# Weight rounding, bank numbers, negated maxima and product buffer of a hybrid trunk kernel rearranged

## What is computed

```python
def mixing_block(h, w_in, mix_out_gain, w_out, ...):
    proj = h @ w_in                                    # 1024 -> all four groups
    u_s5, p_ml, p_rw, p_mb = split_cols(proj, (GW, ML_COLS, RW_COLS, MB_COLS))
    y_s5 = s5_mixer(u_s5, ...)       # complex diagonal scan; y = Re(C x), GLU behind it
    y_ml = mlstm_mixer(p_ml, ...)    # row maxima m, exp(score - m), exp(-m) as a floor
    y_rw = rwkv7_mixer(p_rw, ...)    # token shift of r, k, v; delta rule in time
    y_mb = moba_mixer(p_mb, rel_bias)
    y = rms_norm(jnp.concatenate([y_s5, y_ml, y_rw, y_mb], axis=-1) by group)
    return y @ w_out

def cross_attention(h, mem_n, wq, wkv, wo):
    q = h @ wq
    kv = mem_n @ wkv                                   # mem_n = rms_norm(mem)
    return softmax(q k^T) v @ wo

x = x + rms_norm(mixing_block(rms_norm(x), ...))
x = x + rms_norm(cross_attention(rms_norm(x), rms_norm(mem), ...))
x = x + rms_norm(swiglu(rms_norm(x), ...))
```

## Time and profile before

| | |
|---|---|
| median of 3 runs | 480.02 us |
| lowest, highest | 479.83, 480.71 us |
| the profiled execution | 479.55 us |
| its span in the profile | 477.7 us |
| TensorE busy | 467.7 us (98%) |
| VectorE, ScalarE, GpSimd busy | 345.0, 272.5, 108.4 us |
| mean granted clock of TensorE | 0.997 |

### The profile page before, as it was taken

The page is one execution under the profiler, slowest core; times in us unless marked ns, Lnnn a source line. Parts: engine busy times, 40 slices in busy tenths (PEclk is TensorE's granted clock), DMA queues, the critical chain, the costliest instruction groups (busy, mean ns, idle before and its releaser), DMA issues.

```text
span 477.7 us, 8231 instructions
## 1 busy us (share of the span) xinstructions
PE 467.7 (98%) x3330; PEld 407.4 (85%) x3330; DVE 345.0 (72%) x482; ACT 272.5 (57%) x448; POOL 108.4 (23%) x75
## 2 busy tenths in 40 slices
PE   9999999999999999999999999999999999999995
PEld 6999888988889887889998887888888888888884
DVE  3999999999789987887564747766767777642234
ACT  5778884426334557589366657555555555553332
POOL 0005327793566610000000000000000000444450
PEclk9999999999999999999999999999999999999998
DMA  7884428221411226274633622565554555455502
GB/s 268 331 326 158 173 89 325 69 95 55 149 56 54 90 89 263 90 263 165 233 101 145 238 91 88 184 227 197 206 200 177 176 185 189 169 206 213 185 0 89
DMA packets 12697, 78.91 MB, mean 165 GB/s; under 512 B 1487, under 2 KB 2164, under 8 KB 4084
## 3 DMA queue, kind: packets, MB, share of 16 engines
q1 hardware_dynamic: 12660, 78.39, 45.4%
HBM read 77.33 MB, written 1.84 MB: 166 GB/s over the span
## 4 chain that ended last, share of the span: by engine, by line
PE 74%; DVE 4%; issue 0%; DVEq 0%; ACT 0%
PE bank L415 73%; DVE h L1956 1%; DVE wm_rest L386 1%; DVE wk_rest L386 0%; PE bank L943 0%; PE bank L974 0%; DVE arena L1978 0%; PE bank L653 0%; DVE arena L1899 0%; DVE arena L1969 0%; DVE arena L1979 0%; DVE arena L1927 0%; DVE arena L1925 0%; DVE arena L1898 0%; DVE xres L2146 0%
## 5 line engine op out<-in xcount | busy, mean ns | idle before, releaser
L415 PE MATMUL bank<-h,w_high 128*128 128x512 f32 (+1 forms) x392 | 120.7, 373 | 0.0
L380 ACT ACTIVATE w_high<-ring 128x1024 fp32r<-128x1024 f32 x63 | 66.2, 1058 | 61.2 <-PE bank L415 57.0
L386 DVE TENSOR_TENSOR w_rest<-ring,w_high 128x1024 fp32r<-128x1024 f32 x51 | 63.2, 1245 | 48.8 <-ACT w_high L380 48.6
L415 PE MATMUL bank<-h,w_rest 128*128 128x256 f32 x320 | 89.6, 280 | 0.0
L415 PEld LDWEIGHTS bank<-h,w_high 128*128 128x128 f32 x392 | 68.8, 188 | 13.6 <-issue 0.5
L386 POOL TENSOR_TENSOR w_rest<-ring,w_high 128x1024 fp32r<-128x1024 f32 x7 | 16.8, 2400 | 256.5 <-ACT w_high L380 256.5
L415 PEld LDWEIGHTS bank<-h,w_rest 128*128 128x128 f32 x320 | 60.5, 189 | 0.0
L386 DVE TENSOR_TENSOR w_rest<-third_slot,w_high 128x1024 fp32r<-128x1024 f32 x27 | 32.7, 1223 | 27.3 <-ACT w_high L380 27.2
L415 PE MATMUL bank<-arena 64*64 64x64 f32 (+6 forms) x786 | 50.2, 253 | 2.2 <-POOL arena L1116 1.1
L415 PEld LDWEIGHTS bank<-arena 64*64 64x64 f32 (+3 forms) x786 | 41.8, 144 | 11.3 <-issue 4.6
L415 PE MATMUL bank<-h,we_high 128*128 128x256 f32 x256 | 47.2, 287 | 1.2 <-DVE we_rest L386 0.8
(11 more groups left out here) (346 smaller groups left out, 1038.7 us busy)
## 6 DMA issues: line engine op xcount, KB each, us to landing
ring<-weights SPq DMA_DIRECT2D x49, 1024.0 KB, 4.8
third_slot<-weights SPq DMA_DIRECT2D x15, 1024.0 KB, 4.8
gain<-gains SPq DMA_DIRECT2D x3, 512.0 KB, 5.8
cst<-consts SPq DMA_DIRECT2D x1, 1216.0 KB, 8.6
par<-params SPq DMA_DIRECT2D x1, 1168.0 KB, 10.6
kx<-x_t SPq DMA_DIRECT2D x2, 512.0 KB, 5.7
ring<-weights SPq DMA_DIRECT2D x2, 512.0 KB, 6.6
vx<-mem_t SPq DMA_DIRECT2D x1, 1024.0 KB, 10.0
```

The costliest lines, as they stand in the source:

```text
L380: nc.scalar.activation(split_half(i)[0], raw_half(i), ACT.Copy).then_inc(S["w_high"], 1)
L386: e.tensor_tensor(rest_, raw_half(i), high.bitcast(F32), ALU.subtract).then_inc(rest_done(i)[0], 1)
L415: return nc.tensor.matmul(out_, lhsT, rhs, start=start, stop=stop, skip_group_check=True)
```

## The change

Four things are changed.

1. **Fifth slot.** ScalarE copies the high part of half 9 ahead of the shift of `rw_r`, not behind it, and VectorE makes its rest ahead of the sine argument (L1782).
2. **Banks.** `ml_o` goes to bank 6 instead of 1, A2 to bank 1 instead of 6. A7 stays in 6 and `mb_q` in 1.
3. **Negated maxima.** ScalarE makes `nM` by a copy with scale -1 behind `highs(H_MID + 6)`; VectorE's L1947 is gone. The argument of `em` now raises `ml_em` to 1, ScalarE's exponential waits for that and raises it to 2, and TensorE waits for 2. The copy of `nM` raises `ml_rows`.
4. **Second turn's products.** `prs[1]` lies in `xres`, and GpSimd's wait for `h_rest` 4 is taken out. The transfer of the x rows into `xres` moves from n = 12 to n = 22 of SP's loop, with a wait for the bank `s5_y`, which TensorE fills from the last products.

```diff
--- before.py
+++ after.py
@@ -172,7 +172,7 @@
         sq_x, sq_m = v3(pr_, T), v3(arena[:, at - 512 - 2048 - 2048:at - 512 - 2048], T)
         cos, sin, t1, t2, s5u = (v3(a, T) for a in (cos_, sin_, t1_, t2_, s5u_))
         bu = v4(bu_, 2, T)
-        prs = [v4(pr_, 2, T), v4(flat(vx), 2, T)]
+        prs = [v4(pr_, 2, T), v4(flat(xres), 2, T)]
         (raw_cv, E_, c2n_), at = carve(at, [4 * 259 + 1024, 4 * 384, 256])
         cv = v3(raw_cv[:, 1036:2060], T)
         mlo, mlv = v3(G.rearrange("p a b -> p (a b)"), T), v3(Gp.rearrange("p a b -> p (a b)"), 256)
@@ -754,14 +754,14 @@
                     last = nc.tensor.transpose(o[:, c, j, :], rwM[:, 6 + j, c * P:(c + 1) * P], const("ident"))
             last.then_inc(full[3], 1)
             split_values(7, "ml_v", 0, h_split)
-            split_channel_major(8, "ml_o", 1, h_split)
+            split_channel_major(8, "ml_o", 6, h_split)
 
             pe.wait_ge(S["rw_tilde"], 4)
             for c in range(NC):
                 for h in range(NH):
                     i = c * NH + h
                     r, j = at(h)
-                    b = (4, 5, 6, 7, 0, 2, 3, 6)[i]
+                    b = (4, 5, 1, 7, 0, 2, 3, 6)[i]
                     o = v4(pe_open(pe, f"A{i}", b)[:, :], 2, P)
                     kr = KR[r, :, j, c * P:(c + 1) * P]
                     mm(o[:, 0], Bh[r, j, c * P:(c + 1) * P], kr)
@@ -846,7 +846,7 @@
             attend("num", 2, mlv, E)
             attend("den", 0, None, E)
             o = v3(pe_open(pe, "em", 1)[:, :], T)
-            pe.wait_ge(S["ml_em"], 1)
+            pe.wait_ge(S["ml_em"], 2)
             for j in range(2):
                 last = mm(o[:, j, :], const("pair_sel")[:, j * P:(j + 1) * P], rows[4])
             last.then_inc(full[1], 1)
@@ -1072,6 +1072,8 @@
                     sp.dma_start(mem_h, v3(mem_t, NMEM)).then_inc(S["mem_in"], 16)
                 if n == S_WKV:
                     sp.dma_start(gain_, gain_rows(0)).then_inc(S["gain_in"], 16)
+                if n == S_V6:
+                    wait_full(sp, "s5_y")
                     sp.dma_start(xres, x_rows.rearrange("(m p) c -> p m c", p=P)).then_inc(S["xres_in"], 16)
                 if n == S_FIN:
                     wait_full(sp, f"xs{XH - 1}")
@@ -1155,8 +1157,6 @@
 
                 cq, sq = cos[:, 2 * q:2 * q + 2, :], sin[:, 2 * q:2 * q + 2, :]
                 pool.wait_ge(S["scanned"], q + 1)
-                if q == 1:
-                    pool.wait_ge(S["h_rest"], 4)
                 if q > 1:
                     pool.wait_ge(S["s5_out_used"], 1)
                 for x, (a_, b_) in enumerate(((cq, t1), (sq, t2), (cq, t2), (sq, t1))):
@@ -1325,6 +1325,7 @@
             moved(act, "rw_wag")
             a.activation(rwE[0:HD, 0, 0, :], rwM[0:HD, 0, :], ACT.Tanh).then_inc(S["rw_low"], 1)
             a.activation(rwE[:, 0, 1, :], rwM[:, 1, :], ACT.Tanh, scale=0.5).then_inc(S["rw_exp"], 1)
+            highs(9)
             shifted("rw_r", 2)
             highs(10)
             act.wait_ge(S["theta"], 6)
@@ -1404,7 +1405,10 @@
             level_evac(2)
             highs(H_MID + 5)
             highs(H_MID + 6)
-            act.wait_ge(S["ml_rows"], 3)
+            act.wait_ge(S["ml_row_step"], 3)
+            act.wait_ge(S["zeros_ready"], 2)
+            a.activation(rows[2][0:NH, :], rows[0][0:NH, :], ACT.Copy, scale=-1.0).then_inc(S["ml_rows"], 1)
+            act.wait_ge(S["ml_em"], 1)
             a.activation(rows[4][0:NH, :], rows[4][0:NH, :], ACT.Exp).then_inc(S["ml_em"], 1)
             o = wait_full(act, "g_col")
             a.activation(gcol, o[:, 0:8], ACT.Copy).then_inc(free_of("g_col"), 1)
@@ -1778,9 +1782,9 @@
                 last = v.tensor_scalar(cos[:, i, :], const("time"), frac[:, i:i + 1], ROUND, ALU.mult, ALU.add)
             last.then_inc(S["theta"], 1)
             x_scale("rw_r")
+            rests(9)
             dve.wait_ge(S["theta"], 5)
             v.scalar_tensor_tensor(sin, cos, ROUND, sin, ALU.subtract, ALU.subtract).then_inc(S["theta"], 1)
-            rests(9)
             mix(2, "rw_r")
             x_scale("rw_v")
             rests(10)
@@ -1933,7 +1937,7 @@
 
             dve.wait_ge(S["ml_log"], 3)
             moved(dve, "gates")
-            lf, g_, nM, F, em = (rows[i][0:NH, :] for i in (0, 1, 2, 3, 4))
+            lf, g_, F, em = (rows[i][0:NH, :] for i in (0, 1, 3, 4))
             v.scalar_tensor_tensor(lf, lf, 0.0, F, ALU.min, ALU.subtract).then_inc(S["ml_row_step"], 1)
             dve.wait_ge(S["ml_row_step"], 1)
             one = const("ones", NH)[:, 0:1].to_broadcast([NH, T])
@@ -1944,8 +1948,7 @@
             v.tensor_tensor_scan(lf, g_, g_, 0.0, ALU.max, ALU.max).then_inc(S["ml_row_step"], 1)
             dve.wait_ge(S["ml_row_step"], 3)
             dve.wait_ge(S["zeros_ready"], 2)
-            v.tensor_scalar(nM, lf, -1.0, None, ALU.mult).then_inc(S["ml_rows"], 1)
-            v.scalar_tensor_tensor(em, F, -1.0, lf, ALU.mult, ALU.subtract).then_inc(S["ml_rows"], 1)
+            v.scalar_tensor_tensor(em, F, -1.0, lf, ALU.mult, ALU.subtract).then_inc(S["ml_em"], 1)
 
             project_scaled("mb_k", mqk[:, 2:4, :])
             level_update(2)
```

## The result

The changed kernel takes 484.29 us in the median of four executions (483.42 to 484.61), beside 479.92 us for the kernel before on the same chip; the ratio is 1.0087, with a 95% interval of 1.0074 to 1.0101. It is slower by 4.2 us by the ratio and by 4.4 by the medians. The forecast was slower by 2.1, 482.1 us, and the median lies 0.2 us above the top of the range. The profiled execution took 484.02 us with a span of 482.2, 4.5 more than before.

A forecast was written before the change was run, and what follows sets the result against it. TensorE was taken to bound the kernel, paced by VectorE from 40 to 120 us. The terms -0.7 + 3.5 - 0.7 = +2.1 us on 480.0 gave 482.1 us, range 478.2 to 484.1.

The forecast's parts named there:

- What bounds the kernel: From 40 to 120 us VectorE paces TensorE; after 126 us TensorE hardly waits and a shift is kept to the end.
- Fifth slot: TensorE's 0.76 us wait there goes, but VectorE is 0.7 us late from 39 us; 0.4 of it left in the sum.
- Banks: Output gate and A2 in other banks: cost 0, at most one eviction of 0.42 us, worth nothing further.
- Negated maxima: VectorE's gate rows: gain 1.1 us, less 0.4 of lag, -0.7 us at L1956; bounds -1.3 and +0.3.
- Second turn's products: GpSimd's products take turns with the last four low parts of the memory rows: +3.5 us; bounds 0 and +3.8.
- lost turns: At the last low parts VectorE keeps the interface and GpSimd's products are stretched: 478.0 to 478.6, say 478.4 us; chance 0.27.
- one or two products: Only so many get between the last low parts: 1.2 or 2.4 us instead of 3.5, say 480.4 us; chance 0.18.
- The wait at the fifth level: TensorE's 0.72 us wait at 126.10 for level masks behind GpSimd's products goes: -0.7 us; bounds -0.7 and 0.
- The clock: TensorE's clock falls in the wait before 119.4, products behind run at half speed: costs 1.5, 483.5 us; chance 0.13.
- The range: 478.2 to 484.1 us; the sum's own bounds +1.0 and +4.1, the lower being -1.3 + 3.0 - 0.7.
- Who waits for whom: VectorE with two SBUF inputs and GpSimd share an interface, the second waits for the first; without this, 0 replaces 3.5 us.
- The x rows: Issued near 182 us, in by 194, some 15 us before VectorE adds to them: cost 0.

The follow-up runs named there:

- products alone: Kernel before with only the second turn's products changed (in xres, no wait, x rows late): 484.30 us, ratio 1.0105.
- three products ahead: Kernel before with the second turn's products in xres and x rows late, three of four products free of the wait for h_rest: 481.56 us, ratio 1.0031.
- wait put back: Changed kernel with GpSimd again waiting for h_rest 4 before the second turn's products; x rows still late: 480.01 us, ratio 1.0009.
- all but the fifth slot: Kernel before with the other banks, the maxima on ScalarE and the products change with only one product free of the wait: 478.61 us, ratio 0.9973.
- wait filled: Changed kernel with 29 unneeded matmuls in TensorE's 3.7 us wait before the second half of the keys: 482.87 us, ratio 1.0065.
- two products ahead: Kernel before with the second turn's products in xres and x rows late, two of four products free of the wait for h_rest: 480.00 us, ratio 1.0011.
- one product and maxima: Kernel before with the products change, only the first product free of the wait, and the negated maxima on ScalarE: 478.67 us, ratio 0.9980.
- run cut in two: Kernel before with one product free, maxima on ScalarE, and VectorE's wm_rest moved ahead of the second level's four updates: 478.54 us, ratio 0.9968.
- one product alone: Kernel before with the second turn's products in xres and x rows late, only the first product free of the wait: 478.67 us, ratio 0.9980.

## Why the prediction was right or wrong

**What bounds the kernel, right.** TensorE at the memory rows waits for VectorE, and a shift behind 126 us is kept to the end: +4.44 at 131.75 and +4.5 in the span.

**Fifth slot, right in the mechanism, too small in the size.** The change made VectorE 0.70 us late at 39 us (forecast 0.7). The wait at the fifth slot went and returned in two places, 0.52 us at 37.97, which I had not forecast, and 0.52 at ml_k's second half, 54.11. I let VectorE's lag fall to 0.4 by the idle time at 89 us. In the changed kernel 0.72 are left at the gate rows, the scan of 96.67 there starting at 97.39. The idle time was used, but at 86.9 and 87.9 us the two last scans met a level mask and took 1.08 and 1.06 us instead of 0.66, and the wk_rest of 90.85, only 0.47 late at its start, took 2.19 us beside GpSimd's products instead of 1.94. Alone, without the other banks, the part costs 0.9 us (1.0018), since there TensorE is as late as VectorE at 89 us and the idle time stays.

**Banks, right.** Cost and gain 0 within the error.

**Negated maxima, wrong.** This is the step that failed. The 1.1 us on VectorE are real (L1958 starts 1.10 sooner in the kernel with this part alone; in the changed kernel, with the lag of 0.72, L1959 still starts 0.56 sooner) and none of them arrives at the end of L1956. I had counted the delay only for the next wm_rest, as up to 0.7 us, and taken L1149's 5.39 us as a sign of who loses turns. It had a second meaning: how many of GpSimd's six steps are done before VectorE's long run decides how many are left for the stretch in which the first four low parts stand. One step fewer before it is one more of 1.0 us there: -0.56 at the start of the four becomes +0.45 when TensorE can go on. The forecast had -0.7, with bounds of -1.3 and +0.3.

**Second turn's products, right; the exact size is in part luck.** +3.43 measured, +3.5 forecast, and in the order written down: behind wk_rest three times a product and then a low part. But each turn cost 1.0 us where the forecast had nearly 1.2, and the missing 0.4 came from a level mask beside the last low part, which it didn't have. The prices with two and three products free (1.0 us each) show that it is a price for each product that comes after wk_rest. The rivals of lost turns and of one or two products are out.

**The wait at the fifth level, right.** -0.93 measured, -0.7 forecast; the 0.2 beyond its bound are not explained.

**The clock, wrong in the chance.** It was the rival with 0.13, and its price of 1.5 us is what came: 1.49. The trace of before has no wait of that size ahead of work; its price was an estimate from the 3 us that the tail had left, and that it fitted is luck. In the four executions of the changed kernel and the four with the products alone the mean clock was 0.990 to 0.996, against 0.997 or more in all 73 executions of the kernel before beside the experiments. Why it was 0.990 in four of the eight is not shown. The fastest of the eight, 483.42 us, is slower than the slowest with the clock held, 483.10. A wait of 3.8 us was part of my forecast, and with waits of 3.7 us eight of eight executions show the low mean clock; so the fall belonged in the forecast, on top of the products' 3.5 us, and not in a rival. With it the sum is +3.6; with 1.15 more for the step at the first four low parts (-0.7 became +0.45) and 0.2 less at the fifth level it is +4.5, the difference of the spans. The 1.15 are 1.0 for the step and 0.3 for the lag of the fifth slot, less 0.2 that the shorter gate rows brought more than forecast (1.28 for 1.1). So of the 2.4 us that the forecast lacked the clock is the larger part, 1.5, and the rest is mostly the step. The direction came out right because the largest term did; the size was half of what was measured.

**The range.** Its lower end, 478.2, is called the time of the rival in which GpSimd loses its turns, but that rival was worked out as 478.0 to 478.6. And the 3.0 us for the products in the lower bound of the sum have no source. Neither decided anything here: the measured time lies at the other end.

**Who waits for whom.** The Trainium skill, page "SBUF — State Buffer", section "Who interferes with whom", says that a VectorE operation with two SBUF inputs and a GpSimd operation that reads SBUF block one another, and that the order of issue decides which waits. That the second of the two waits for all of the first is what the rows at 118 to 122 us show, 1.49 for 0.41 us. That the order of issue decides who waits holds there too, and doesn't hold at 100.97 us, where GpSimd's step began 0.64 us before wm_rest and, at 1.3 us alone, should have ended at 102.3; it ended at 106.2, behind all of VectorE's run (the start times of GpSimd are those of the profile, which is rough there):

```profile
100.97 5.27 POOL L1150 TENSOR_TENSOR arena<-arena 128x512 f32<-128x512 f32 x1
101.61 1.21 DVE L386 TENSOR_TENSOR wm_rest<-ring,wm_high 128x1024 fp32r<-128x1024 f32 x1
```

**The x rows, right.** Issued at 186.61 us, landed 9.7 us later, and first needed by VectorE at 215.66.

## What to carry to other kernels

A wait that looks like lost time on an idle engine may be what keeps it out of the way of the engine on the critical path: before taking it out, write down turn by turn what the freed work will stand beside. Here the right amount was one product of four, beside work that reads banks; all four cost 3.4 us and one wins 1.0. And a new wait of TensorE is to be priced twice, once for itself and once for the slow clock that may follow: 1.5 us behind 3.7 us each time, and behind 1.2 to 2.3 us in some executions, where it cost 0 to 1.3. The cause of a gain that doesn't arrive may be a few instructions further: here one GpSimd step of 1.3 us that fell out of one stretch and into the next.

## What the runs showed of the hardware

The clock can fall after TensorE has begun to work again, not during its wait: 1.00 in the 3.6 us of standing still, 0.59 and then 0.50 behind it. 29 matmuls of no use in the wait kept it at 1.00 and won 1.1 to 1.4 us. Whether it falls behind a shorter wait differs between executions of one program. Only the profiled executions show where it fell; for the others the table counts a mean clock of 0.996 or less, which no execution with shorter waits at the keys had:

| longest wait at the keys | kernel | executions with a fall |
|---|---|---|
| 3.7 us | changed; products alone | 8 of 8 |
| 2.30 us | three products ahead | 4 of 9 |
| 1.38 us | wait put back | 3 of 10 |
| 1.38 us | all but the fifth slot | 2 of 6 |
| 1.38 us | wait filled | 0 of 4 |
| 1.24 us | two products ahead | 3 of 10 |
| 1.11 to 1.14 us | maxima alone; one product and maxima; run cut in two | 0 of 26 |
| 0.66 us | fifth slot, banks or one product alone | 0 of 30 |
| 0.66 us | before, beside the experiments | 0 of 73 |

A GpSimd operation can stand for a whole run of VectorE's operations with two SBUF inputs, 5.3 us for one that takes 1.3, though by the profile it began first. Cutting the run cut the hold. Elsewhere the two engines take turns one for one, and what decides between the two is open.
